# More conv taps in the attention slots, a rotated key over 128 rows, ones ahead of the first tiles, and the conv norm's variance summed onto all partitions

## The reference, cut to what matters

```
u = a * sigmoid(g)
u = causal_depthwise_conv(u, conv_w, conv_b)        # 31 taps, 1024 channels
u = silu(layernorm(u, conv_ln_g, conv_ln_b))        # mean and variance over the 1024 channels
q_pe = apply_rope(q_pe, cos, sin)                   # 64 of a head's 192 columns
k_pe = apply_rope(k_rope, cos, sin)                 # one rotated key, shared by all 8 heads
attn = causal_attention(concat(q_nope, q_pe), concat(k_nope, k_pe), v)
mix = concat([rmsnorm(u, conv_out_norm), rmsnorm(attn, attn_out_norm)]) @ w_out
x = x + rmsnorm(mix, post_mix_norm)
```

## Time and profile before

| | us |
|---|---|
| median of three runs (lowest, highest) | 2229.53 (2223.72, 2231.84) |
| the profiled execution, its own time | 2224.91 |
| its span on the core | 2223.2 |
| PE busy, DVE busy, ACT busy, POOL busy | 2186.4, 1289.1, 1109.2, 50.1 |

### The profile page before, as it was taken

The page is one execution under the profiler, slowest core; times in us unless marked ns, Lnnn a source line. Parts: engine busy times, 40 slices in busy tenths (PEclk is TensorE's granted clock), DMA queues, the critical chain, the costliest instruction groups (busy, mean ns, idle before and its releaser), DMA issues.

```text
span 2223.2 us, 28777 instructions
## 1 busy us (share of the span) xinstructions
PE 2186.4 (98%) x10134; PEld 1817.7 (82%) x10134; DVE 1289.1 (58%) x1660; ACT 1109.2 (50%) x1461; POOL 50.1 (2%) x59
## 2 busy tenths in 40 slices
PE   8999989999999999999999999999999999999999
PEld 6897767888888888888888877888888888888887
DVE  5898757544554455444465556665565656565443
ACT  5546644544444444444357345655665656554333
...
GB/s 218 191 184 156 128 99 152 188 189 190 189 188 188 189 189 207 191 196 189 185 150 157 171 120 130 142 187 183 185 190 181 180 197 175 194 169 208 193 192 162
DMA packets 216097, 393.11 MB, mean 177 GB/s; under 512 B 13679, under 2 KB 57785, under 8 KB 215771
## 3 DMA queue, kind: packets, MB, share of 16 engines
...
q10 hardware_dynamic: 176, 1.06, 0.1%
...
## 4 chain that ended last, share of the span: by engine, by line
PE 93%; DVE 4%; ACT 1%; SPq 1%; issue 1%; POOL 0%; DMA 0%; DVEq 0%; ACTq 0%; POOLq 0%
PE ps L507 29%; PE ps L509 29%; PE ps L508 29%; DVE cv L1799 1%; DVE w_lo L1699 1%; PE ps L1079 1%; PE ps L523 1%; PE ps L797 0%; PE ps L907 0%; PE ps L926 0%; DVE fac L2098 0%; PE ps L642 0%; PE ps L643 0%; PE ps L744 0%; PE ps L753 0%
## 5 line engine op out<-in xcount | busy, mean ns | idle before, releaser
L1699 DVE TENSOR_TENSOR w_lo<-raw,w_hi 128x1024 fp32r<-128x1024 f32 (+2 forms) x761 | 899.9, 1191 | 773.6 <-ACT w_hi L1123 769.7
L1123 ACT ACTIVATE w_hi<-raw 128x1024 fp32r<-128x1024 f32 (+2 forms) x761 | 777.7, 1030 | 721.4 <-PE ps L509 683.2
L507 PE MATMUL ps<-w_hi,hT_hi 128*128 128x512 f32 (+2 forms) x2208 | 866.9, 393 | 13.3 <-DVE w_lo L1699 8.0
L509 PE MATMUL ps<-w_hi,hT_lo 128*128 128x512 f32 (+2 forms) x2208 | 855.2, 387 | 0.0
L508 PE MATMUL ps<-w_lo,hT_hi 128*128 128x512 f32 (+2 forms) x2208 | 854.7, 387 | 0.0
L507 PEld LDWEIGHTS ps<-w_hi,hT_hi 128*128 128x128 f32 x2208 | 416.3, 189 | 97.2 <-issue 11.6
L509 PEld LDWEIGHTS ps<-w_hi,hT_lo 128*128 128x128 f32 x2208 | 416.3, 189 | 80.3
L508 PEld LDWEIGHTS ps<-w_lo,hT_hi 128*128 128x128 f32 x2208 | 416.7, 189 | 76.2
L507 PE MATMUL ps<-w_hi,aT_hi 128*128 128x512 f32 x704 | 274.0, 389 | 0.0
L509 PE MATMUL ps<-w_hi,aT_lo 128*128 128x512 f32 x704 | 273.9, 389 | 0.0
L508 PE MATMUL ps<-w_lo,aT_hi 128*128 128x512 f32 x704 | 273.9, 389 | 0.0
...
## 6 DMA issues: line engine op xcount, KB each, us to landing
...
```

The costliest lines, as they stand in the source:

```text
L507: pe.matmul(o, xh, wh, start=first, stop=False)
L509: mm = pe.matmul(o, xl, wh, start=False, stop=last)
L1123: act.activation(w_hi[:, s, :kc, :width], raw[:, s, :kc, :width], ACT.Copy).then_inc(hi_ready, 1)
L1699: dve.tensor_tensor(w_lo[:, s, :kc, :width], raw[:, s, :kc, :width], w_hi[:, s, :kc, :width].bitcast(F32), ALU.subtract).then_inc(lo_ready, 1)
```

## The change

The change has four parts:

1. `SLOT_TAPS` is raised from 66 taps in the slots to 88: one more in slots 1 to 3, three more in slots 4 to 10, one less in slots 12 and 13. The run behind the slots has 4 taps in place of 26.
2. The rotated key is stored with 64 columns of zeros on both sides and transposed twice, once for even and once for odd heads, so that `kpeT` is 128 x 2 x 256 with the unused half zero. L643 then reads all 128 rows. The tile `kpe` moves into the space of `attn1`.
3. PE issues 8 matmuls of ones before anything else, and 6 more after the first transposes of x; the first column block of x is loaded as two halves, each ahead of a weight tile.
4. The variance is summed by 8 products against ones of 128 x 256 (`sums_spread`), which put it on all partitions. DVE scales it as 128 x 256, POOL raises it to the power -1/2 as 128 x 256, and DVE multiplies `cv` with that. The diagonal and the second spread (L1916, L761) are gone. ACT and DVE split tiles in another place around it.

```diff
+START_WARM = 8, 6
-SLOT_TAPS = [2, 4, 5, 5] + [5] * 10
+SLOT_TAPS = [2, 5, 6, 6] + [8] * 7 + [5, 4, 4]
...
+            for n in range(2):
+                sp.dma_start(x_sb[:, :, cols(n, GW)], x_in[:, :, cols(n, GW)]).then_inc(x_landed[n], 16)
                 load_gate(0, n)
+            for n in range(1, 4):
+                sp.dma_start(x_sb[:, :, cols(n)], x_in[:, :, cols(n)]).then_inc(x_landed[n + 1], 16)
+                if n < 3:
+                    load_gate(0, n + 1)
...
+                if name == "ln":
+                    pool.tensor_tensor(lnsq[:, 1, :], lnsq[:, 0, :], minus_half[:, 0:1].to_broadcast([P, SEQ]),
+                                       ALU.pow).then_inc(rstd_ready, 1)
+                    continue
...
             pe.wait_ge(consts_ready, 1)
+            keep_warm(START_WARM[0], 1)
...
+            keep_warm(START_WARM[1], 1)
             pe.wait_ge(gains_ready, 1)
...
-                    mm = pe.matmul(o, qpeT[r, h // 2, t * P:(t + 1) * P], kpeT[r, 0:n], start=False, stop=True)
+                    mm = pe.matmul(o, qpeT[:, h // 2, t * P:(t + 1) * P], kpeT[:, e, 0:n], start=False, stop=True)
...
+            def sums_spread(bank, src):
+                for c in range(CC):
+                    mm = pe.matmul(ps[:, bank, 0:SEQ], ones[:], src[:, c, :], start=(c == 0), stop=(c == CC - 1))
+                mm.then_inc(ln_mm, 1)
...
                 if g == LN_VAR:
                     pe.wait_ge(ln_act, 1)
-                    column_sums(5)
-                if g == LN_SPREAD:
-                    pe.wait_ge(ln_dve, 2)
-                    for t in range(TOK):
-                        mm = pe.matmul(ps[:, 4, t * P:(t + 1) * P], ones[:], lnsq[:, 0, t * P:(t + 1) * P],
-                                       start=True, stop=True)
-                    mm.then_inc(ln_mm, 1)
+                    sums_spread(5, lnsq)
...
-            act.activation(kpeT[:, :], ps[:, 5, 0:SEQ], ACT.Copy).then_inc(kpe_ready, 1)
+            act.activation(kpeT[:].rearrange("p e s -> p (e s)"), ps[:, 5, :], ACT.Copy).then_inc(kpe_ready, 1)
...
             dve.wait_ge(ln_mm, 2)
-            mean_sq("ln", CONV, ps[:, 5, 0:TOK])
+            dve.tensor_scalar(lnsq[:, 0, :], ps[:, 5, 0:SEQ], 1.0 / CONV, EPS, ALU.mult, ALU.add).then_inc(ms_ready, 1)
             dve.wait_ge(rstd_ready, r_count("ln"))
-            for t in range(TOK):
-                ins = dve.tensor_scalar(lnsq[:, 0, t * P:(t + 1) * P], ident[:], r_of(rstd, "ln", t, 1), None, ALU.mult)
-            ins.then_inc(ln_dve, 1)
-            lo_upto(T_OUT1 + LN_SPREAD + 2)
-            dve.wait_ge(ln_mm, 3)
-            spread = ps[:, 4, 0:SEQ].unsqueeze(1).to_broadcast([P, CC, SEQ])
-            dve.tensor_tensor(cv[:], spread, cv[:], ALU.mult).then_inc(ln_dve, 1)
+            dve.tensor_tensor(cv[:], cv[:], lnsq[:, 1, :].unsqueeze(1).to_broadcast([P, CC, SEQ]), ALU.mult).then_inc(ln_dve, 1)
             lo_upto(T_OUT1 + 18)
```

More of the change, by code:

```diff
@@ L100 @@
 SLOT_TILE0 = T_UKV + 2
-SLOT_TAPS = [2, 4, 5, 5] + [5] * 10
+SLOT_TAPS = [2, 5, 6, 6] + [8] * 7 + [5, 4, 4]
 ATT_END = [7, 8, 12, 16]
-LN_MEAN, LN_VAR, LN_SPREAD, MIX_VAR = 10, 12, 13, 18
+LN_MEAN, LN_VAR, MIX_VAR = 10, 12, 18
 T_FF1 = _phase(2 * FB, [2] * 8, lambda b: NB)
@@ L227, in build @@
         sg_s = attn1[:, :, NB:2 * NB]
+        kpe = attn1[:, :, 0:3 * ROPE]
+        pos = kpeT[:, 0, 0:TOK].bitcast(I32)
         raw_landed = [sem(f"raw_landed{s}") for s in range(RING)]
@@ L233, in build @@
         tp_ready, tp_hi, tp_free = sem("tp_ready"), sem("tp_hi"), sem("tp_free")
-        x_landed = [sem(f"x_landed{n}") for n in range(4)]
+        x_landed = [sem(f"x_landed{n}") for n in range(5)]
         params_landed, late_landed, grow_landed, out_landed = (
@@ L358, in load_gate @@
                     sp.dma_start(raw[:, s, :, cols(i, GW)], w_in[:, 2 * n:2 * n + 2, at:at + GW]).then_inc(raw_landed[s], 16)
-            for n in range(4):
-                sp.dma_start(x_sb[:, :, cols(n)], x_in[:, :, cols(n)]).then_inc(x_landed[n], 16)
+            for n in range(2):
+                sp.dma_start(x_sb[:, :, cols(n, GW)], x_in[:, :, cols(n, GW)]).then_inc(x_landed[n], 16)
                 load_gate(0, n)
+            for n in range(1, 4):
+                sp.dma_start(x_sb[:, :, cols(n)], x_in[:, :, cols(n)]).then_inc(x_landed[n + 1], 16)
+                if n < 3:
+                    load_gate(0, n + 1)
             small_loads()
@@ L550, in _ @@
             for n in range(2):
-                pe.wait_ge(x_landed[0], 16)
+                pe.wait_ge(x_landed[n], 16)
                 fill(F_XT1 + n, x_sb, n)
+            keep_warm(START_WARM[1], 1)
             pe.wait_ge(gains_ready, 1)
@@ L557, in _ @@
                 if n < 6:
-                    pe.wait_ge(x_landed[n // 2 + 1], 16)
+                    pe.wait_ge(x_landed[n // 2 + 2], 16)
                     fill(F_XT1 + n + 2, x_sb, n + 2)
@@ L634, in attn1_S @@
             def attn1_S(h):
-                e, r = h % 2, slice(ROPE * (h % 2), ROPE * (h % 2) + ROPE)
+                e = h % 2
                 pe.wait_ge(at_qk, h + 1)
@@ L716, in _ @@
                     pe.wait_ge(kpe_ready, 1)
-                    for t in range(TOK):
-                        mm = pe.transpose(ps[:, 5, t * P:(t + 1) * P], kpe[:, t, :], ident[:])
+                    for e in range(2):
+                        for t in range(TOK):
+                            at = ROPE * (1 - e)
+                            mm = pe.transpose(ps[:, 5, e * SEQ + t * P:e * SEQ + (t + 1) * P], kpe[:, t, at:at + 2 * ROPE],
+                                              ident[:])
                     mm.then_inc(kpe_ready, 1)
@@ L751, in _ @@
                     pe.wait_ge(tp_free, F_MIX1 + HEADS)
-                    for c in range(CC):
-                        mm = pe.matmul(ps[:, 4, 0:SEQ], ones[:], cv[:, c, :], start=(c == 0), stop=(c == CC - 1))
-                    mm.then_inc(ln_mm, 1)
+                    sums_spread(4, cv)
                 if g == LN_VAR:
                     pe.wait_ge(ln_act, 1)
-                    column_sums(5)
-                if g == LN_SPREAD:
-                    pe.wait_ge(ln_dve, 2)
-                    for t in range(TOK):
-                        mm = pe.matmul(ps[:, 4, t * P:(t + 1) * P], ones[:], lnsq[:, 0, t * P:(t + 1) * P],
-                                       start=True, stop=True)
-                    mm.then_inc(ln_mm, 1)
+                    sums_spread(5, lnsq)
                 if g == MIX_VAR:
@@ L1170, in _ @@
             hi_upto(9)
-            for n in range(4):
+            for n in range(5):
                 act.wait_ge(x_landed[n], 16)
@@ L1334, in _ @@
             attn_half(2)
-            hi_upto(T_OUT1 + LN_SPREAD + 3)
-            act.wait_ge(ln_dve, 3)
+            hi_upto(T_OUT1 + LN_VAR + 4)
+            act.wait_ge(ln_dve, 2)
             for c in range(CC):
@@ L1765, in _ @@
             dve.wait_ge(gains_ready, 3)
-            step(dve.tensor_copy(posf[:, 0, :], kpe[:, 0, 0:TOK].bitcast(I32)))
+            step(dve.tensor_copy(posf[:, 0, :], pos))
             tt = [trig_t[:, i, :].rearrange("p (t n) -> p t n", t=TOK) for i in range(4)]
@@ L1853, in _ @@
                     dve.wait_ge(tp_free, F_LAT + 5)
-                    step(rope(kpe[:, :, 0:ROPE].unsqueeze(2), z1[:, :, QL + KVL:Z1].unsqueeze(2), 32, 1, 0,
-                              [t[:, :, 0:1, :] for t in tmp]))
-                    dve.tensor_copy(kpe[:, :, ROPE:2 * ROPE], kpe[:, :, 0:ROPE]).then_inc(kpe_ready, 1)
+                    dve.memset(kpe[:, :, 0:ROPE], 0.0)
+                    dve.memset(kpe[:, :, 2 * ROPE:3 * ROPE], 0.0)
+                    rope(kpe[:, :, ROPE:2 * ROPE].unsqueeze(2), z1[:, :, QL + KVL:Z1].unsqueeze(2), 32, 1, 0,
+                         [t[:, :, 0:1, :] for t in tmp]).then_inc(kpe_ready, 1)
                 if g == 67:
@@ L1933, in _ @@
             lo_upto(T_OUT1 + 20)
-            dve.wait_ge(ln_mm, 4)
+            dve.wait_ge(ln_mm, 3)
             mean_sq("conv", CONV, ps[:, 5, 0:TOK])
```

8 lines of the change are left out of this document (4 added, 4 removed).

## The result

The changed kernel takes 2249.41 us (median of 4 runs, 2245.99 to 2250.58) against 2226.93 us (4 runs) for the kernel before: ratio 1.0098, 95% interval 1.0077 to 1.0119. It is slower by 22.5 us. The profiled execution took 2245.99 us, with a span of 2244.2.

The account below looks back on a forecast made before the run. PE, 98% busy, bounds the kernel. +27.1 (power and variance, with the taps' gain) + 0.9 (start) + 0 (key) = +28.0 us on 2224.9 gives 2252.9, placed at 2255; own range 2238 to 2275, 8 in 10 2236 to 2287.

Parts of the forecast that it names:

- The power (part 4): POOL's power on 128 x 256 variances: priced per column, 0.16 us each on 0.38 fixed, 41 us; chance 0.70.
- 1.66 plus a delay: POOL's old 8-column powers, 2.39 us: the per-column line gives 1.66, the other 0.73 read as a delay per instruction.
- Rival B: POOL's variance power slower, no delay in the 8-column rows: 72 us, kernel 2284 us (88 would be 2300); chance 0.12.
- rival C: POOL's variance power has a start-up, then a third of the price per column: about 14 us, kernel 2227; chance 0.06.
- rival A: POOL's variance power as quick as its multiplication, 0.74 us: kernel faster, 2211.5 or 2214 us; chance 0.12.
- whatever the arithmetic: Skill's POOL rule as the prediction read it: 2.6 cycles per element for any operation, so the power 0.55 us plus fixed part.
- What follows it: Behind POOL's power: DVE waits, splits queue behind it, PE idles 40 us from 296.2 to 336.1; a loss of 27.1 us.
- 8 to 14: PE after the long wait for the power: this many matmuls at the 1.2 GHz level, 1.6 to 2.8 us more.
- The taps (part 1): DVE's taps moved into the slots: PE's 7.8 us wait goes, PE doesn't wait in slots, mean's sums 3.5 us at full clock.
- The start (part 3): PE's first tiles: gain given back waiting at tile 3, start about 0.5 us later; +0.9 us taken, between 0 and 2.1.
- The chain was the one named: Before tile 3: ACT waits for weight tile 4's DMA, issued by SP after all small loads; one DMA more, about 0.5 us later.
- The rotated key (part 2): Score products on 128 rows cost the same as on 64, extra transposes and copies covered by PE's wait: 0 us.

Follow-up runs that it names:

- the repeat on 8 columns: Kernel before plus nine scratch POOL instructions at its start: powers on 2 to 64 columns, 8 and 2 repeated, and a multiplication; 2223.87 us, one run.
- the three orders with four, two and no changes: Score products per head: kernel before (128, 64, 128, 64 rows), 2225.9 us; reordered 128, 64, 64, 128, 2224.59 us; rotated key alone, all 128, 2221.59 us.

## Why the prediction was right, and where it was off

**The power (part 4): right in kind and in size.** 0.38 + 256 x 0.16 = 41 us was predicted, 41.13 measured. The reading of the 8-column rows as 1.66 plus a delay held: the repeat on 8 columns took 1.63. Rival B, the same rows read as a steeper price, falls with it; rival C, a start-up and then a lower slope, falls with the equal slopes; rival A would have been right for a multiplication (0.61). The Trainium skill, GPSIMD Engine Reference, "Performance versus the Vector engine", gives about 2.6 cycles per element for a two-input elementwise instruction, measured on an addition. It does not name the power, so "whatever the arithmetic" in the prediction was more than the page says. The multiplication comes near the page's figure (0.61 us in all against the 0.55 estimated from it, without a fixed part; from 64 to 256 columns (0.61 - 0.29) / 192 = 1.7 ns per column, where the figure gives 2.2), the power does not (160 ns).

**What follows it: right.** PE idle from 291.0 to 330.77, 39.7 us (predicted 40). From the start of the mean's sums to tile 16 the prediction had 302.9 + 41 - 278.2 = 65.7 us, and 338.44 - 272.95 = 65.5 were measured. Ten matmuls at half clock behind the wait, of "8 to 14".

**The taps (part 1): right.** The wait of 7.8 us gone, the sums at clock 1.00 in 3.72 us (predicted 3.5), PE not held in the slots. Alone the part gains 9.7 us.

**The start (part 3): right in size, not in the place of the wait.** Tile 3 started at 23.43 instead of 22.97, 0.46 us later; predicted 0.5 for that and 0.9 placed. The chain was the one named: SP issued weight tile 4 at 15.93 instead of 15.58, and ACT began its split at 20.27 instead of 19.81. But the prediction had PE wait at tile 3 for what it had gained. PE was through with tile 0 at 11.5 instead of 15.2, 3.7 us sooner (forecast 2 to 3), and gave most of that back before tile 1 and in it: timeline of PE in the changed kernel, tiles 1 and 3:

```profile
14.87 0.79 PE L518 MATMUL ps<-w_hi,hT_hi 128*128 128x512 f32 x1 [2.77 <-DVE hT_lo L1738]
...
23.43 0.50 PE L518 MATMUL ps<-w_hi,hT_hi 128*128 128x512 f32 x1 [0.55 <-DVE hT_lo L1738]
```

It waited 2.77 us for the split activations of tile 1 and then ran at a granted clock of 0.52 (14.80 to 18.00); at tile 3 its wait is 0.55 us, as before. In the kernel with the start alone it was as forecast, 2.29 us of waiting at tile 3. In all kernels with the changed start and the old order of loads tile 3 began at 23.43 to 23.97, with the old start at 22.81 to 23.17 in six and 23.77 in a seventh.

**The rotated key (part 2): wrong in size; this is the mis-sized term.** The prediction said "the score products take the same columns on 128 rows as on 64: 0". Beside neighbours of their own row count the products do cost the same (0.59 and 0.60 us). The sum left out the changes from one row count to the other: four per head at 0.18 us, 0.73 us per head and 5.8 us over eight heads. The 2.08 us of a head were in the trace before; the step went wrong in pricing a product by its columns and not by its neighbours. The Trainium skill, TensorEngine Tiling (Array Packing), "Key Properties", says that a change of the tiling mode drains the engine. Products on 64 rows of the array beside products on 128 fit that rule, and the three orders with four, two and no changes agree with it, at the price above, as do the weight loads, which at a change start only with their product; more of a drain than that no run here shows. It was the rule that spoke against a cost of 0, and the prediction didn't weigh it. PE's shorter scores also shortened DVE's wait for them, from 12.0 us in seven times to 7.0 with the key alone; in the changed kernel, with the added taps in that place, it is 1.5.

**The sum.** The forecast was 2255 us and the median measured 2249.4, inside both ranges. Predicted was +28.0 against the profiled execution, measured 2245.99 - 2224.9 = +21.1. Of the 6.9 us between them 5.8 are the key, 0.4 the start; 0.4 lie behind tile 16 and the rest, 0.3, is in small differences that I can't assign, and that are no larger than what executions differ by: the start of the mean's sums varied by 1.7 us between four kernels that are alike up to there (272.95, 274.10, 274.68, 273.77).
